# Latent attention's output projection as three products of rounded halves

## The reference

```python
def mla_mixer(hc, hx, row, col, w_in, q_norm_g, w_uq, kv_norm_g, w_ukv, w_out):
    ...
    return out(yc, xsc, zc), out(yx, xsx, zx)   # gated by silu, then @ w_out

x = x + gx * yx
if i < DEPTH - 1:
    ctx = ctx + gc * yc
```

## Time and profile before

| What | Value |
|---|---|
| Median of 3 runs | 1979.32 us (1978.59 to 1980.76) |
| The profiled execution | 1980.76 us, span 1979.0 us |
| PE busy | 1880.8 us, 95% of the span |
| VectorE, ScalarE, GpSimd busy | 1243.6, 696.1, 130.4 us |
| Mean granted clock of PE | 0.975 of 2.4 GHz |
| Latent attention's heads, on PE | 1521 to 1686 us |
| Output projection and sums of squares | 1686.69 to 1748.76 us |

### The profile page before, as it was taken

How to read it: one execution, slowest core, us unless ns; L and a number is a source line. 1 busy time by engine, 2 the same in 40 slices (tenths; PEclk the granted TensorE clock), 3 DMA queues, 4 the chain that set the end, 5 groups by cost and what they waited for, 6 DMA issues and landing times.

```text
span 1979.0 us, 30724 instructions
## 1 busy us (share of the span) xinstructions
PE 1880.8 (95%) x13040; PEld 1592.9 (80%) x13040; DVE 1243.6 (63%) x2232; ACT 696.1 (35%) x929; POOL 130.4 (7%) x68
## 2 busy tenths in 40 slices
PE   6999999998999989998999989998999998989997
PEld 4999988877999989998888789998744555436896
DVE  3887655535887687665672469997794665125712
ACT  2433243233533263334332363332521333024322
POOL 0000063300000000004430000000000000000000
PEclk9999999989999999999999999999999998999999
DMA  9777623422577646663334037765351201112100
GB/s 391 286 271 260 236 107 128 172 86 107 219 260 287 242 161 242 250 237 140 135 137 184 22 149 274 278 247 203 110 209 64 86 1 66 45 62 85 65 22 22
DMA packets 47256, 323.81 MB, mean 164 GB/s; under 512 B 4960, under 2 KB 8160, under 8 KB 8336
## 3 DMA queue, kind: packets, MB, share of 16 engines
q1 hardware_dynamic: 47120, 321.85, 43.0%
HBM read 320.78 MB, written 1.05 MB: 163 GB/s over the span
## 4 chain that ended last, share of the span: by engine, by line
PE 86%; DVE 8%; ACT 3%; issue 1%; SPq 1%; DMA 1%; DVEq 0%; ACTq 0%
PE ps L336 85%; DVE wk L1778 3%; ACT wk L1298 2%; DVE wk L1775 2%; PE ps L339 1%; DVE wk L1772 1%; SPq L1274 1%; DVE low L1772 1%; DMA ring<-in_stream_dram 1%; ACT L1298 1%; DVE xa L1775 0%; DVE xlo L1772 0%; DVE tab L1772 0%; ACT xa L1298 0%; DVE wk L1781 0%
## 5 line engine op out<-in xcount | busy, mean ns | idle before, releaser
L336 PE MATMUL ps<-xa,ring 128*128 128x256 f32 (+1 forms) x1776 | 485.5, 432 | 18.2 <-ACT xa L1298 11.6
L336 PEld LDWEIGHTS ps<-xa,ring 128*128 128x128 f32 x1776 | 338.6, 193 | 150.7 <-issue 103.9
L336 PE MATMUL ps<-xhi,low 128*128 128x256 f32 x1408 | 387.9, 283 | 0.0
L336 PE MATMUL ps<-xhi,whi_wk 128*128 128x256 f32 x1088 | 306.9, 293 | 19.3 <-ACT xhi L1298 12.4
L1298 ACT ACTIVATE wk<-ps 128x256 f32<-128x256 f32 (+4 forms) x221 | 109.8, 504 | 583.0 <-PE ps L336 497.7
L336 PE MATMUL ps<-xlo,whi_wk 128*128 128x256 f32 x1088 | 297.5, 282 | 0.0
L336 PEld LDWEIGHTS ps<-xhi,low 128*128 128x128 f32 x1408 | 262.9, 190 | 0.0
L1298 ACT ACTIVATE whi_wk<-ring 128x2048 fp32r<-128x2048 f32 x100 | 191.0, 1914 | 201.7 <-DMA ring<-in_stream_dram 115.0
L1778 DVE SCALAR_TENSOR_TENSOR wk<-ring,sc,wk 128x256 f32<-128x256 f32 x576 | 234.0, 477 | 0.0
L336 PE MATMUL ps<-wk 64*64 64x64 f32 (+10 forms) x2712 | 223.4, 270 | 6.7 <-ACT wk L1298 5.1
L1772 DVE TENSOR_TENSOR low<-ring,whi_wk 128x2048 fp32r<-128x2048 f32 x100 | 228.1, 2284 | 0.3 <-ACT whi_wk L1298 0.3
(11 more groups left out here) (108 smaller groups left out, 2404.9 us busy)
## 6 DMA issues: line engine op xcount, KB each, us to landing
ring<-in_stream_dram SPq DMA_DIRECT2D x302, 1024.0 KB, 5.9
tab<-in_tab_dram SPq DMA_DIRECT2D x1, 1376.0 KB, 24.0
res<-in_xt_dram SPq DMA_DIRECT2D x1, 1024.0 KB, 23.1
res<-in_ct_dram SPq DMA_DIRECT2D x1, 1024.0 KB, 8.7
out_dram<-wk SPq DMA_DIRECT2D x2, 512.0 KB, 3.0
tab<-in_tab_dram SPq DMA_DIRECT2D x1, 256.0 KB, 2.9
cols<-in_cols_dram SPq DMA_DIRECT2D x1, 242.5 KB, 2.6
tab<-in_wg_dram SPq DMA_DIRECT2D x1, 96.0 KB, 2.0
```

The costliest lines, as they stand in the source:

```text
L336: last[0] = nc.tensor.matmul(o, l, r, start=start, stop=stop, skip_group_check=free)
```

## The change

- PE makes 24 products of 128 x 512 for each output tile in place of 8: high weights x high half, low weights x high half, high weights x low half of the heads' outputs, for k from 0 to 7, of type float32r.
- Each weight chunk takes two places of the ring (`take_both`). The second has no transfer of its own: the loaded chunk lies in the first, ScalarE writes its rounded copy to the second (`out_high`), and VectorE replaces the loaded chunk by the low half (`out_low`). The projection's four chunks so fill the ring. Both places are released together.
- ScalarE copies each gated pair `xa[:, t]`, rounded, to `o_hi` (`heads_high`) and VectorE replaces `xa[:, t]` by its low half (`heads_low`), in rounds 3, 5, ..., 15 for t = 0 to 6, and after the loop for t = 7. The weights' copies stand in rounds 12, 13, 14 and after the loop, their subtractions in rounds 13, 14, 15 and after the loop.
- PE's wait for all gated pairs is replaced by a wait for the chunk's low half, and in the first output tile by one for each pair's low half.

```diff
+            def take_both(*tag):
+
+                held[0] = n = len(order)
+                found[("chunk_no",) + tag] = ("", n)
+                order.append(tag)
+                order.append(("rounded",))
+                return n
...
             def release():
 
                 last[0].then_inc(tensor_done, 1)
                 done.named("chunk", held[0])
+                if held[0] + 1 < len(order) and order[held[0] + 1] == ("rounded",):
+                    found["chunk", held[0] + 1] = found["chunk", held[0]]
...
-                eng.wait_ge(vector_done, step("o_read", 7))
...
                 for ch in range(4):
-                    w = tiles(take("wout2", 0, ch), 256)
+                    no = take_both("wout2", 0, ch)
+                    hi, lo = tiles(low[:, (no + 1) % RING, :], 256), tiles(low[:, no % RING, :], 256)
+                    eng.wait_ge(vector_done, step("olow", ch))
...
+                        at = slice(P * t, P * t + P)
                         for k in range(KT):
-                            mm(bank(b), w[:, k, P * t:P * t + P], xa[:, k, :], k == 0, k == KT - 1, free=True)
+                            if n == 0:
+                                eng.wait_ge(vector_done, step("ol", k))
+                            mm(bank(b), hi[:, k, at], heads_hi(k), k == 0, False, free=True)
+                            mm(bank(b), lo[:, k, at], heads_hi(k), False, False, free=True)
+                            mm(bank(b), hi[:, k, at], whi_xa[:, k, :], False, k == KT - 1, free=True)
...
-            for n in range(stream.shape[0]):
+            rows = 0
+            for n, tag in enumerate(order):
+                if tag == ("rounded",):
+                    continue
...
+                def heads_high(t):
+
+                    eng.wait_ge(vector_done, step("o_read", t))
+                    act(heads_hi(t), xa[:, t, :], ACT.Copy, "oh", t).then_inc(scalar_done, 1)
+
+                def out_high(ch):
+
+                    n = found["chunk_no", "wout2", 0, ch][1]
+                    eng.wait_ge(landed[n % RING], loads(n))
+                    eng.wait_ge(*step_of("chunk", n + 1 - RING))
+                    act(low[:, (n + 1) % RING, :], ring[:, n % RING, :], ACT.Copy, "oround", ch).then_inc(scalar_done, 1)
...
+                    if h > 2 and h % 2:
+                        heads_high((h - 3) // 2)
+                    if 12 <= h < 15:
+                        out_high(h - 12)
+                heads_high(7)
+                out_high(3)
...
+                def heads_low(t):
+
+                    eng.wait_ge(scalar_done, step("oh", t))
+                    tt(whi_xa[:, t, :], xa[:, t, :], heads_hi(t).bitcast(F32), SUB, "ol", t).then_inc(vector_done, 1)
+
+                def out_low(ch):
+
+                    n = found["chunk_no", "wout2", 0, ch][1]
+                    eng.wait_ge(scalar_done, step("oround", ch))
+                    tt(low[:, n % RING, :], ring[:, n % RING, :], low[:, (n + 1) % RING, :].bitcast(F32), SUB, "olow", ch).then_inc(vector_done, 1)
...
+                    if h > 2 and h % 2:
+                        heads_low((h - 3) // 2)
+                    if 13 <= h < 16:
+                        out_low(h - 13)
+                heads_low(7)
+                out_low(3)
```

More of the change, by code:

```diff
@@ L130, in build @@
         hlo = nc.alloc_sbuf_tensor_at("hlo", [P, 4, T], F32R, offset=wk_at + 4 * (SCR + 8960 + 4 * T))
+        o_hi = nc.alloc_sbuf_tensor_at("o_hi", [P, 6, 2 * T], F32R, offset=wk_at + 4 * 20480)
+        o_hi2 = nc.alloc_sbuf_tensor_at("o_hi2", [P, 2, 2 * T], F32R, offset=wk_at + 4 * 10240)
         PS = ctx.enter_context(nc.psum_tensor("ps", [P, 8, 512], F32))
@@ L148, in step_of, with loads, heads_hi @@
             return (signals[marks[key][0]], marks[key][1]) if marks else (vector_done, 1)
+        def loads(n):
+            return 16 * sum(1 for i in range(n % RING, n + 1, RING) if order[i] != ("rounded",))
+        def heads_hi(t):
+            return o_hi[:, t, :] if t < 6 else o_hi2[:, t - 6, :]
         def bank(b, lo=0, hi=512):
@@ L353, in take @@
                 order.append(tag)
-                eng.wait_ge(landed[n % RING], 16 * (n // RING + 1))
+                eng.wait_ge(landed[n % RING], loads(n))
                 return ring[:, n % RING, :]
+            def take_both(*tag):
[4 more added lines that the diff above has]
+                return n
             def release():
@@ L1270, in _ @@
             wg_after = found["chunk_no", "gla_in", 0][1]
-            for n in range(stream.shape[0]):
+            rows = 0
+            for n, tag in enumerate(order):
+                if tag == ("rounded",):
+                    continue
                 if n >= RING:
                     eng.wait_ge(*step_of("chunk", n - RING))
-                eng.dma_start(ring[:, n % RING, :], stream[n]).then_inc(landed[n % RING], 16)
+                eng.dma_start(ring[:, n % RING, :], stream[rows if marks else 0]).then_inc(landed[n % RING], 16)
+                rows += 1
                 if n == GATE - 2:
@@ L2627 @@
     _, (marks, order) = program(1, None)
+    order = [tag for tag in order if tag != ("rounded",)]
     nc, _ = program(len(order), marks)
```

## The result

The changed kernel takes 1968.1 us (median of 4 runs, 1967.53 to 1969.99), the kernel before 1979.9 us (4 runs). The ratio of the changed kernel's time to that of the kernel before is 0.9943, with a 95% interval of 0.9925 to 0.9960. Forecast were 1969.1 us and faster. The profiled execution takes 1969.99 us with a span of 1968.1 us, 10.9 us less than before.

The account below looks back on a forecast made before the run. PE was taken to bound the output projection. Terms -13.4 (products), +3.9 (late heads), -0.8 (start wait) and +0.1 (earlier rounds) sum to -10.2 us, from the median 1979.32 to 1969.1 us; range 1965.3 to 1974.3.

Parts of the forecast that it names:

- The products: Output projection on PE: 64 fp32 products become 192 passes of 0.216 us, 41.5 us in place of 54.9, gain 13.4.
- rival 1: Projection: a pass costs 0.235 us, the extra growing with the columns; gain only 9.8 us, 1972.7 us in all; chance 10%.
- Rival 3: Projection: weight loads not hidden behind products, 0.320 us a pass, 61.4 us for 192, 1989.0 us in all; chance 4%.
- Rounds 3 to 12: Heads' loop: five short VectorE subtractions in rounds 3 to 11 mostly covered by slack of some 0.68 us; cost 0.1 us.
- Rounds 13 to 16: Late heads' loop: subtractions delay round 14's weighted sum by 3.3 us, then 0.3, 0.1 and 0.2 for the clock.
- the late heads: Last rounds of the heads' loop: added VectorE work and a lower clock cost 3.9 us, from 0.5 to 6.5.
- Rival 2: Heads' loop: all VectorE subtractions lie on the path and cost 14.3 us, 1979.4 us in all; chance 7%.
- Rival 4: Last head: the clock is up there, so the added work costs 0.7 us, 1965.9 us in all; chance 9%.
- The wait at the start: Projection's start: PE's 0.78 us wait for the last pair's gated output goes, as seven pairs' products come first; 0.8 us gained.
- the ring: Weight ring: second places delay the next stage's first chunk load, but it is covered; cost nothing, 5.9 us once if not.

Follow-up runs that it names:

- narrow_weights: Changed kernel with each of the 192 products taking only 64 weight columns and writing 64 partitions, half the outputs left out; one execution, 1972.84 us.
- bf16: Changed kernel with the rounded and low halves of weights and heads in bfloat16 instead of float32r; 1966.82 us, ratio 0.9934 to the kernel before.
- lows_later: Changed kernel with VectorE's subtractions for weight chunks 0, 1, 2 moved to round 15, round 16 and behind the loop; 1966.84 us, ratio 0.9938.
- all_in_gaps: As lows_later, with the heads' short subtractions also moved to the next even round, between VectorE's copy and its scaling; 1967.26 us, ratio 0.9936.

## Why the prediction was right, and where not

**The products.** The step that failed is the size of a pass: "512 + 6 cycles ... 0.216 us". It is 0.2328 us, 559 cycles, so the projection took 44.7 us and not 41.5, and gained 10.35 us and not 13.4 (rival 1 had 0.235 and 9.8). The reason given for the smaller value, that the weights fill the extra cycles at 256 columns and are covered at 512, fails at 512 by narrow_weights and bf16: the extra is 26 cycles at 256 columns and 47 at 512 (9 to 10%), it is 6 with bfloat16 at 512, and half the load takes 5 or 6 away. What fills the 26 cycles at 256 columns no run tests. The nearest row should have been scaled and not explained away: rival 1, which had a chance of 10%, did that and has the mechanism.

**The load beside the stream.** Rival 3 is out: 0.2328 us is far under stream and load together, 0.320. The Trainium skill, TensorE: Matmul & The Clock Gate, The mechanism, says in its list that weight loads overlap running products only when the row group differs; that does not hold here. The section's first paragraph also lets a load into the background weight buffer go early, which no run here tests. The same page of the Trainium skill, Back-to-back issue gap, gives N / 2.4 + 2.5 ns; 215.8 ns for 512 columns agrees with the bfloat16 pass (0.2159 us) and not with the float32r one.

**Rounds 3 to 12.** Forecast 0.1 us, measured 0.8: in the heads' rounds 4, 8 and 12 PE's weighted sum slipped by 0.38, 0.24 and 0.2 us more against the kernel before (1566.48 and 1606.79 against 1566.34 and 1606.41, with the heads' start 0.23 earlier, make 0.37 and 0.61 together). The slack was overrated: from the end of VectorE's copy (1606.43) to PE's start are 0.36 us, where 0.15 was assumed. Rows 8 and 9 had shown it: ahead of round 14's weighted sum the same copy ends at 1663.26 and PE starts at 1663.58, 0.32 later.

**Rounds 13 to 16.** Forecast 3.3 us at round 14's weighted sum and 3.9 in all. Measured is +3.97 us there, 0.8 of it from rounds 3 to 12, and then -1.2 us up to the projection, -0.8 of which is the removed wait and the rest the clock. So the late heads cost 2.8 us, not 3.9: the clock gave back 0.4 where it was to cost 0.2, and two subtractions cost less than was put for them. Loop and end together, with rounds 3 to 12 and the removed wait, are also +2.8 us, against a forecast of +3.2. lows_later and all_in_gaps show the mechanism: one long subtraction ahead of the maxima, and the short ones, the one of round 13 at its whole length. The small costs forecast for the long ones of round 14 (0.3) and 15 (0.1) are not there. From that round's weighted sum to the last turning are 13.76 us (1667.32 to 1681.08), against 13.58 in lows_later without the subtraction, but the 0.18 us are already lost at the turning ahead of it, in a stretch in which PE runs on without a wait and the granted clock is lower (7.27 us at 0.74 against 7.09 at 0.76, 5.4 at the full clock in both). From that turning to the last one are 6.49 us in both. Rival 2 is out: of 14.3 us on VectorE about 4 lay on the path. Rival 4 is out too: the last turning took 2.62 us and the weighted sum behind it 4.37, where 1.48 and 2.81 would have been the high clock.

**The wait at the start and the ring.** Both as forecast: no wait ahead of the first product or in the projection, 8.68 us from the sums to the next layer in both.

**The total.** 3.1 us less from the products, 0.4 us more from loop and end, and 3.1 us from the second layer's clock, which the forecast did not have: two misses of the same size cancelled. That the median came out within 1 us of the forecast is luck. Without the second layer the profiles give 7.6 us, 1972.3 from the median before, which is inside the range, 3 us from the point and close to the 1972.7 of rival 1. The three timed comparisons lie, by their ratios, 9.5 to 11.3 us under the kernel before; what they have beyond 7.6 is not shown to belong to the change.

## What to carry to other kernels

Price a fast product by its nearest relative of the same type, scaled, and do not carry the overhead of another type over to it. Work that is hidden in the sum of an engine's busy time is free only in a place where that engine waits: the same subtraction costs up to its whole length ahead of the maxima and nothing between the copy and the scaling, where the wait for the exponentials covers it. Where the clock moves a stage by 3 us between executions of one kernel, compare stage by stage, not total by total.

## What the hardware showed that was not expected

- A back-to-back float32r product of 512 columns takes 0.2328 us at a granted clock of 1.00, a bfloat16 one 0.2159, half an fp32 record 0.2145. Three float32r passes cost 0.698 us where one fp32 product costs 0.858.
- Half as many weight columns shorten a float32r pass by 0.002 us; the same weights twice in a row by nothing, and a DMA share of 0.93 beside it lengthens it by nothing (0.2324 and 0.2322 us).
- The clock falls to 1.2 GHz within a stage in which PE is never idle: in the second layer's start it is 0.90 or 0.95 of full speed with the same records (65.8 and 62.7 us), without any change of the kernel. In the first profile of the kernel before one such fall, at 1773.77, comes behind eight records of 16x512 (1769.16 to 1772.79), and PE has no idle time in between; whether those records bring it about is not tested.
